# Router products from the rows of X, with the norm put in around them, and the first piece's subtraction in two halves

## The reference, cut to what matters

```python
def rmsnorm(x, g):
    y = xf * lax.rsqrt(jnp.mean(xf * xf, axis=-1, keepdims=True) + EPS)
    return y * g

x = x + mix @ w_out[l]
h = rmsnorm(x, ffn_norm[l])                 # l = 1
logits = h @ router                         # (256, 1024) @ (1024, 8)
top_val, top_idx = lax.top_k(logits, 2)     # experts of each token
gates = softmax(top_val)
hid = silu(xb @ w_gate[e]) * (xb @ w_up[e]) # xb: the tokens of one expert
y[token] += (hid @ w_down[e]) * gate
```

## Time and profile before

| | us |
|---|---|
| median of 3 runs | 1515.6 |
| lowest and highest | 1512.71, 1517.51 |
| the profiled execution, whole time | 1515.23 |
| its span in the trace | 1513.5 |
| mean granted clock of TensorE over the span | 0.987 of full |
| beginning of the expert loop's products in the trace | 548.0 |
| beginning of the second piece's products | 551.58 |

### The profile page before, as it was taken

How to read it: one execution, slowest core, us unless ns; L and a number is a source line. 1 busy time by engine, 2 the same in 40 slices (tenths; PEclk the granted TensorE clock), 3 DMA queues, 4 the chain that set the end, 5 groups by cost and what they waited for, 6 DMA issues and landing times.

```text
span 1513.5 us, 20687 instructions
## 1 busy us (share of the span) xinstructions
PE 1480.0 (98%) x7788; PEld 1237.6 (82%) x7788; DVE 1160.3 (77%) x917; ACT 956.8 (63%) x881; POOL 160.1 (11%) x131
## 2 busy tenths in 40 slices
PE   6999999999999999999999999999999999999997
PEld 6977699998987578888888888888888888888876
DVE  4783455555685378888889888888888889888896
ACT  4454344444555167777777777777777777777764
POOL 5222000000130242000000000000000000000480
PEclk9999999999999989999999999999999999999999
DMA  8536556644433179999999999999999999999992
GB/s 264 201 112 219 198 195 199 232 126 155 138 112 112 68 258 396 394 392 390 386 374 382 386 372 378 391 376 375 394 370 372 394 377 362 395 394 358 399 389 112
DMA packets 212311, 450.19 MB, mean 297 GB/s; under 512 B 12932, under 2 KB 37032, under 8 KB 212264
## 3 DMA queue, kind: packets, MB, share of 16 engines
q1 hardware_dynamic: 211112, 445.35, 80.8%
q0 software_dynamic: 1152, 4.19, 0.7%
HBM read 435.36 MB, written 14.16 MB: 297 GB/s over the span
## 4 chain that ended last, share of the span: by engine, by line
PE 94%; DVE 2%; ACT 2%; issue 1%; DMA 0%; POOL 0%; SPq 0%; DVEq 0%; POOLq 0%; ACTq 0%
PE bank L1545 27%; PE bank L1547 27%; PE bank L1546 27%; PE bank L1841 2%; PE bank L1825 2%; PE bank L1939 2%; DVE low L1391 1%; PE bank L1656 1%; PE bank L1559 1%; DMA gain<-in_attn_norm_dram 0%; PE bank L1927 0%; PE bank L1695 0%; PE bank L1723 0%; PE bank L1552 0%; ACT high L1017 0%
## 5 line engine op out<-in xcount | busy, mean ns | idle before, releaser
L1391 DVE TENSOR_TENSOR low<-raw,high 128x2048 fp32r<-128x2048 f32 x336 | 775.4, 2318 | 108.7 <-ACT high L1017 108.5
L1017 ACT CAST high<-raw 128x2048 fp32r<-128x2048 f32 x336 | 644.0, 1917 | 180.5 <-PE bank L1547 180.5
L1545 PE MATMUL bank<-high,xeh 128*128 128x512 f32 x896 | 353.9, 395 | 2.7 <-DVE low L1391 2.7
L1547 PE MATMUL bank<-high,xel 128*128 128x512 f32 x896 | 349.5, 390 | 0.0
L1546 PE MATMUL bank<-low,xeh 128*128 128x512 f32 x896 | 348.9, 389 | 0.0
L1545 PEld LDWEIGHTS bank<-high,xeh 128*128 128x128 f32 x896 | 168.3, 188 | 37.5 <-DVE low L1391 3.9
L1547 PEld LDWEIGHTS bank<-high,xel 128*128 128x128 f32 x896 | 168.2, 188 | 35.9
L1546 PEld LDWEIGHTS bank<-low,xeh 128*128 128x128 f32 x896 | 168.4, 188 | 33.6
L1545 PE MATMUL bank<-high,hdh 128*128 128x512 f32 x448 | 175.2, 391 | 1.5 <-DVE low L1391 1.5
L1547 PE MATMUL bank<-high,hdl 128*128 128x512 f32 x448 | 174.4, 389 | 0.0
L1546 PE MATMUL bank<-low,hdh 128*128 128x512 f32 x448 | 174.4, 389 | 0.0
(11 more groups left out here) (316 smaller groups left out, 1977.3 us busy)
## 6 DMA issues: line engine op xcount, KB each, us to landing
raw<-in_moe_w_gate_dram SPq DMA_DIRECT2D x112, 1024.0 KB, 7.5
raw<-in_moe_w_up_dram SPq DMA_DIRECT2D x112, 1024.0 KB, 7.8
raw<-in_moe_w_down_dram SPq DMA_DIRECT2D x112, 1024.0 KB, 7.5
ring<-in_w_in_dram SPq DMA_DIRECT2D x10, 2048.0 KB
dring<-in_dense_w_gate_dram SPq DMA_DIRECT2D x5, 2048.0 KB
dring<-in_dense_w_up_dram SPq DMA_DIRECT2D x5, 2048.0 KB
dring<-in_dense_w_down_dram SPq DMA_DIRECT2D x5, 2048.0 KB
ring<-in_w_in_dram SPq DMA_DIRECT2D x8, 1024.0 KB, 7.4
```

What stands on the lines that cost most here:

```text
L1017: act.copy(high[:, q % SPLIT, :], raw[:, q % RAW, :]).then_inc(s_hi, 1)
L1391: dve.tensor_tensor(low[:, q % SPLIT, :], raw[:, q % RAW, :], high[:, q % SPLIT, :].bitcast(F32), ALU.subtract).then_inc(s_lo, 1)
L1545: pe.matmul(o, xh, wh, start=first, stop=False)
L1547: return pe.matmul(o, xl, wh, start=False, stop=last)
```

## The change

Six edits, five of which belong together:

1. The norm's weights of the second mixer are loaded as 8 more rows of PR (a third small DMA), turned and copied with the others, so that PC has 44 columns, and DVE multiplies the router by them once, in layer 0 (step k = 7).
2. `turn(3, t, n)` turns X, not XN, and waits for the residual, not for the norm.
3. On PE the second tile's first half is turned ahead of `router_logits(0)`, the second half behind it; the three `keep_running` products between are gone; the logits go to bank 6 and wait for `hT` half by half. On ACT the copy of that first half stands ahead of the last `square_sum`.
4. DVE's first step of the choice multiplies the logits by the tokens' scales, in place of a copy.
5. GAP_CHOICE is 6, not 14.
6. `piece_low(0, 0)` is made in two halves: one behind RT_DIFF, one behind the selection of the first job.

```diff
-    GAP_NORM, GAP_DENSE, GAP_CHOICE = 10, 6, 14
+    GAP_NORM, GAP_DENSE, GAP_CHOICE = 10, 6, 6
...
+                        sp.dma_start(PR[GAINS0:NROWS, :], ffn_norm[1, :].rearrange("(k p) -> k p", p=P)).then_inc(s_rows, 16)
...
                 for n in range(2):
                     turned_copy(2 * l + 1, dst, 0, n)
+                if l:
+                    turned_copy(2 * l + 1, dst, 1, 0)
                 square_sum(2 * l + 1, 1, 1)
-                for n in range(2):
+                for n in range(l, 2):
                     turned_copy(2 * l + 1, dst, 1, n)
...
+                    if l == 0 and k == 7:
+                        dve.wait_ge(s_rw, 16)
+                        dve.wait_ge(s_pc, 1)
+                        dve.tensor_tensor(RW[:, :, :], RW[:, :, :], bc(PC[:, GAINS0:NROWS].unsqueeze(2), [P, KD, NE]),
+                                          ALU.mult).then_inc(s_rwg, 1)
...
-            piece_low(0, 0)
...
             dve.wait_ge(s_lg, 1)
-            then(dve.tensor_copy(RT[:, 0, :], ps[7][:, 0:16]))
+            dve.wait_ge(s_rms, T * 4)
+            then(dve.tensor_tensor(row(0), ps[6][:, 0:16].rearrange("p (t e) -> p t e", t=T),
+                                   bc(st[:, 3, 1, :].unsqueeze(2), [P, T, NE]), ALU.mult))
...
+            piece_low(0, 0, 0, PIECE // 2)
             dve.wait_ge(s_rk, 1)
...
             select(0, lambda t: first_slot[:, t:t + 1])
+            piece_low(0, 0, PIECE // 2)
...
-                pe.wait_ge(s_xn, 4 * i + 2 * t + n + 1)
+                if i == 2 * DEPTH - 1:
+                    pe.wait_ge(s_res, 8 * (DEPTH - 1) + 2 * t + n + 1)
+                else:
+                    pe.wait_ge(s_xn, 4 * i + 2 * t + n + 1)
+                rows_ = X if i == 2 * DEPTH - 1 else XN
...
-                pe.wait_ge(s_rw, 16)
-                pe.wait_ge(s_res, 12)
-                pe.wait_ge(s_hT, 2 * t + 2)
+                pe.wait_ge(s_rwg, 1)
+                pe.wait_ge(s_res, 10)
                 for k in range(KD):
-                    ins = pe.matmul(ps[7][:, t * NE:(t + 1) * NE], hT[:, k, t * P:(t + 1) * P], RW[:, k, :],
+                    if k % 4 == 0:
+                        pe.wait_ge(s_hT, 2 * t + k // 4 + 1)
+                    ins = pe.matmul(ps[6][:, t * NE:(t + 1) * NE], hT[:, k, t * P:(t + 1) * P], RW[:, k, :],
                                     start=(k == 0), stop=(k == KD - 1))
...
                     pe.matmul(ps[0][:, 0:2], ident[:, :], UO[:, 0:2], start=True, stop=True).then_inc(s_used, SPLIT)
+                    turn(2 * l + 1, 1, 0)
                     router_logits(0)
-                keep_running(0, (GAP_NORM, GAP_NORM // 3)[l])
-                for n in range(2):
-                    turn(2 * l + 1, 1, n)
+                    turn(2 * l + 1, 1, 1)
```

More of the change, by code:

```diff
@@ L175, in bass_hybrid_trunk_kernel @@
         G2f = G2[:, :, :, :].rearrange("p t h d -> p (t h d)")
-        NROWS = DEPTH * CK * 4 + 4
+        GAINS0 = DEPTH * CK * 4 + 4
+        NROWS = GAINS0 + KD
         PR = G2f[0:NROWS, 512:640]
@@ L268, in bass_hybrid_trunk_kernel @@
         s_rw = sem("router_loaded")
+        s_rwg = sem("router_scaled")
         w_loaded = [sem(f"slot{i}_loaded") for i in range(RING)]
@@ L513, in _ @@
                         gate_biases(0)
-                        sp.dma_start(PR[0:NROWS - 4, :], mlstm_conv.rearrange("l j (c p) -> (l j c) p", p=P)).then_inc(s_rows, 16)
-                        sp.dma_start(PR[NROWS - 4:NROWS, :], hgrn_lb.rearrange("l (c p) -> (l c) p", p=P)).then_inc(s_rows, 16)
+                        sp.dma_start(PR[0:GAINS0 - 4, :], mlstm_conv.rearrange("l j (c p) -> (l j c) p", p=P)).then_inc(s_rows, 16)
+                        sp.dma_start(PR[GAINS0 - 4:GAINS0, :], hgrn_lb.rearrange("l (c p) -> (l c) p", p=P)).then_inc(s_rows, 16)
+                        sp.dma_start(PR[GAINS0:NROWS, :], ffn_norm[1, :].rearrange("(k p) -> k p", p=P)).then_inc(s_rows, 16)
                     if l == 0 and i == 1:
@@ L1386, in _, with piece_low @@
                             add_residual(t, n)
-            def piece_low(j, q):
+            def piece_low(j, q, c0=0, c1=PIECE):
                 dve.wait_ge(s_hi, nth_piece(j, q))
-                dve.tensor_tensor(low[:, q % SPLIT, :], raw[:, q % RAW, :], high[:, q % SPLIT, :].bitcast(F32),
-                                  ALU.subtract).then_inc(s_lo, 1)
-            piece_low(0, 0)
+                ins = dve.tensor_tensor(low[:, q % SPLIT, c0:c1], raw[:, q % RAW, c0:c1], high[:, q % SPLIT, c0:c1].bitcast(F32),
+                                        ALU.subtract)
+                if c1 == PIECE:
+                    ins.then_inc(s_lo, 1)
             def select(j, rows):
@@ L1555, in turn @@
             def turn(i, t, n):
-                pe.wait_ge(s_xn, 4 * i + 2 * t + n + 1)
+                if i == 2 * DEPTH - 1:
[3 more added lines that the diff above has]
+                rows_ = X if i == 2 * DEPTH - 1 else XN
                 for c in range(4):
                     ins = pe.transpose(ps[TURN_BANKS[i][2 * t + n]][:, c * P:(c + 1) * P],
-                                       XN[:, t, (4 * n + c) * P:(4 * n + c + 1) * P], ident[:, :])
+                                       rows_[:, t, (4 * n + c) * P:(4 * n + c + 1) * P], ident[:, :])
                 ins.then_inc(s_xt, 1)
@@ L1739, in _ @@
                 if l == 0:
-                    pe.wait_ge(s_rows, 16 * 2)
+                    pe.wait_ge(s_rows, 16 * 3)
                     pe.transpose(ps[6][:, 0:NROWS], PR[:, :], ident[0:NROWS, 0:NROWS]).then_inc(s_prT, 1)
@@ L1847, in _ @@
                     pe.matmul(ps[0][:, 0:2], ident[:, :], UO[:, 0:2], start=True, stop=True).then_inc(s_used, SPLIT)
+                    turn(2 * l + 1, 1, 0)
                     router_logits(0)
-                keep_running(0, (GAP_NORM, GAP_NORM // 3)[l])
-                for n in range(2):
-                    turn(2 * l + 1, 1, n)
-                if l == 0:
+                    turn(2 * l + 1, 1, 1)
+                else:
+                    keep_running(0, GAP_NORM)
+                    for n in range(2):
+                        turn(2 * l + 1, 1, n)
                     def down(i):
```

## The result

The changed kernel takes 1512.14 us (median of 12 runs, 1504.17 to 1513.22), the kernel before 1517.4 beside it (12 runs, 1512.65 to 1517.91). The ratio is 0.9962, with a 95% interval of 0.9947 to 0.9978: 0.38% faster, 5.8 us, of which the interval leaves 3.3 to 8.0 (the two medians differ by 5.3). The forecast was 1511.1 us in a range of 1508.6 to 1514.6.

What follows compares the result with a forecast made beforehand. PE, busy 98% of the span, bounds the kernel, so only an earlier expert loop counts: second piece 4.3 us earlier, less 0.2 for layer 0, makes 4.1, so 1515.2 becomes 1511.1 us, range 1508.6 to 1514.6.

Steps and rivals of the forecast that it cites:

- PE up to the logits: PE from the small product's end at 525.68 through turns and router products: logits at 531.6 us, before 535.12.
- The scales: Normalisation on DVE done at 530.0, before the logits at 531.6, hence free; 0.5 us to spare with a high clock.
- Keepers 2.8 for six: Six keep-running products ahead of the ranks take 2.8 us at half clock, ending 534.4, about when the choice is ready.
- Ranks 2.3 at the low clock: Ten rank products on PE after the choice take 2.3 us at half clock, from 534.4 to 536.8.
- Half subtraction 1.23: DVE's first half subtraction, 534.5 to 535.7, costs 1.23 us and hides behind the ranks at half clock.
- The gather: PE's gather after the selection begins at 537.8, 4.7 us earlier.
- From the gather to the second piece 9.5: Gather's start to second piece takes 9.5 us, before 9.07; 0.4 to 0.5 of the second half subtraction's 1.23 shows.
- Layer 0: The extra small load and DVE's router multiplication in layer 0 cost nothing, at most 0.2 us, which was put in.
- The clock rule: On PE the low clock is the default and activity releases it; fewer keep-running products then mean a longer low stretch.
- The rival that I drew from it: Low clock through the gather, 1512.5 to 1515 (0.21 with a late-DVE case), or on into the expert loop (0.05).
- rival A: High clock throughout from logits to gather: second piece at 545.1, 6.5 us earlier, total 1508.9; chance 0.24.
- rival C: Low clock goes on into the expert loop, each piece more costing 2.7: one gives 1517.4, two 1520; chance 0.05.

Runs made afterwards that it cites:

- router_only: Changed kernel with 14 keep-running products again and the whole first subtraction ahead of the choice, leaving the router's part; ratio 0.9983, stretch 21.7 us.
- behind_choice: Changed kernel with the whole first subtraction behind RT_DIFF, none behind the selection; ratio 0.9966, stretch 20.9 us.
- no_halves: Changed kernel with the whole first subtraction ahead of the choice again; ratio 0.9979, stretch 22.9 us.
- halves_only: Kernel before with only the first piece's subtraction split in two, behind RT_DIFF and behind the selection; ratio 1.0011, stretch 26.6 us.
- gap_zero: Changed kernel with no keep-running products ahead of the ranks instead of 6; ratio 0.9966, stretch 20.8 us.
- gap_only: Kernel before with only GAP_CHOICE changed, 6 keep-running products ahead of the ranks instead of 14; ratio 1.0004, stretch 26.0 us.
- no_gap: Changed kernel with 14 keep-running products ahead of the ranks again instead of 6; ratio 0.9972, stretch 22.7 us.
- gap_and_halves: Kernel before with 6 keep-running products and the subtraction in two halves, without the router's part; ratio 1.0006, stretch 24.7 us.

## Why the prediction was right, point by point

- **Where the gain is.** All of it lies between the output projection and the second piece, 5.5 of the 5.6 us, as said. The rest of the span is 961.8 against 961.9.
- **PE up to the logits: right in order, 1 us too long.** The step that was off is the term for the second tile's router products, put at 3.1 (528.5 to 531.6). They took 2.19. I let the clock fall at 529.1 because it had fallen there before; it fell at 529.5, with ten of sixteen products done, and at the high clock a product takes 0.105 in an unbroken row, not 0.12. In two other traces (router_only, behind_choice) the clock stayed high through all of them, 1.75.
- **The scales.** Free in this case, as said. With the clock high they are nearly on the path: in behind_choice DVE goes from the normalisation to the choice with 0.19 of waiting. I had allowed 0.5.
- **Keepers 2.8 for six**: 2.76. **Ranks 2.3 at the low clock**: 2.33 from the first to `first_slot`. **Half subtraction 1.23**: 1.23, hidden.
- **The gather** began at 536.6, forecast 537.8. The 1.2 are the 1.0 above and 0.2 of small steps.
- **From the gather to the second piece 9.5**: 9.52, over the second half subtraction, as said. no_halves and halves_only confirm the price.
- **Layer 0.** The multiplication took 0.22, and DVE's wait for ACT behind it shrank from 0.34 to 0.21:

```profile
96.11 0.22 DVE L1305 TENSOR_TENSOR RW<-RW,PC 128x64 f32<-128x64 f32 x1
...
97.82 2.29 DVE L1109 TENSOR_TENSOR winl<-ring,winh 128x2048 fp32r<-128x2048 f32 x1 [0.21 <-ACT winh L827]
```

  The stretch began at 525.43 against 525.40, and from the first product of layer 0's long unbroken row (27.48 against 27.40) to there it is 497.95 against 498.00. The 0.2 that I had put in were not needed.
- **The clock rule.** The rule that I had set beside the rows, in the Trainium skill, "TensorE: Matmul & The Clock Gate", section "Part 1: The HAM clock gate (the "warmup" mystery)", is that activity releases the low clock. The traces agree: in the stretch of all fourteen the clock rose within a row of PE products or as one ended. The rival that I drew from it, that eleven fewer keepers mean a longer low stretch, does not hold for the changed kernel: the clock was low for 10.2 us in its stretch and for twice 3.4 in its second trace, for 10.2 and once more 3.4 in that of before, and for 10.2 with no keepers ahead of the ranks at all (gap_zero). The one trace of gap_only is as the rival has it, with 17.1 us.
- **Total.** Step by step the sum gave 4.3 and the trace 5.45: the 1.0 of the router products and 0.1 to 0.2 of small steps. This trace went the way of my forecast, low from about 529 and high again in the gather. The second trace did not: its gain of 6.7 is that of rival A, with a clock that was low in two places where it cost little. That the measured 1512.1 lies only 1.0 from the forecast is in part luck: I started from a profiled execution of 1515.2, while the median of before beside the result is 1517.4, and these 2.2 us were partly made good by a gain that was 1.2 us larger than forecast (5.3 against 4.1). The chances put a gain over 0.3% at 0.47 and "within 0.3%" at 0.50; the measured 0.38% is on the side that I held for slightly less likely, and the interval reaches across the border. In rival C the time for one more piece is 0.2 too low by its own terms (1514.9 + 2.7 = 1517.6), which moves nothing in the forecast.

What was not tried: the turns out of X without the new order on PE, and the other way round. The two are one edit in all runs, so how they share the gain of router_only is open.

## What to carry to other kernels

Edits on one chain are not worth what they are worth alone. Here the two small ones gave +0.2 and -0.5 us by themselves and about 2 each once the logits came earlier (one trace each); each frees a queue that matters only when the wait ahead of it is gone, so try them together and undo them one by one. Filler products that keep an engine's clock up stand in its queue like any others: size them by when the next real work is ready, and size them anew when that moves. And work moved out of one wait goes to wherever its engine is idle in the new trace, with the second half of what does not fit still on the path.

## What the runs showed of the hardware

**More than half of the spread ahead of the stretch arises in the first 30 us.** The time up to the stretch was 521.3, 524.1, 525.4 or 528.2 us in kernels that hardly differ there. The first gate products show why. This is the kernel before (timeline of PE):

```profile
14.87 1.06 PE L1630 MATMUL bank<-WG,hTh 128*128 128x32 f32 x8 [0.68 <-ACT hTh L769]
```

and this is no_gap, the same products half a microsecond later:

```profile
15.35 1.89 PE L1648 MATMUL bank<-WG,hTh 128*128 128x32 f32 x8 [0.68 <-ACT hTh L772]
17.08 1.85 PE L1652 MATMUL bank<-WG,hTl 128*128 128x16 f32 x8
```

The turns ahead of them are the same instructions. In the one execution the clock is high here until 17.1 and low for 6.8 us from there, in the other it stays low to about 27: the long unbroken row of products behind them begins at 27.40 and at 30.17, so 2.8 us are lost. Over all fourteen traces it begins between 26.4 and 30.3. The other 3 us of the spread come from two low stretches of 3.4 us each, at about 65 and about 420, of which each costs some 1.5: both are missing in gap_and_halves (521.3), the second in router_only and behind_choice (524.1 and 524.2). The spread of 12 runs, 5 us for before and 9 us for the changed kernel, is of this size, and is the reason why a gain of 5.5 us in one trace needs a dozen runs to be seen in the median. A stretch of the trace that the edit touches, between two points that all kernels share, told the same with one trace each, to about 1 us.

**The windows can show 1.00 where the clock was low.** In no_gap, the stretch of 17.6 to 22.0 is given as

```profile
17.60:22.00 4.40, 4.40 (x23) 4.40 (x22) 4.11 (x2) 1.29 (x1) 4.25 (x3) 1.00 1.00 286
```

while 8 products take 1.85, as they do at 0.50 elsewhere. Ahead of the first change of clock that the trace has on record there is nothing to read; the length of equal products is what tells.

**A small shift is answered by the clock.** The low stretches there lasted from 3.4 to 17.1 us, and where they begin moves against the kernel: in the two traces of the changed kernel the clock fell 4.1 and 4.5 us behind the stretch's beginning, with the ranks at the low clock in the one and nearly all of them at the high one in the other, 20.7 against 19.5 us of stretch. In router_only and behind_choice it fell only 13.1 and 9.6 us behind it. A step that is some tenths sooner or later may therefore gain or lose 1 us more by the clock, whatever its own length. That is the margin which an estimate such as this one has to carry.
